# Up products of a weight chunk in two runs of one width each, and another order of the last twelve blocks of down products

## The reference

```python
# first block: one layer, D_FF = 4096
h2 = rmsnorm(x, g_mlp[i])
u = jax.nn.relu(jnp.einsum("bsd,df->bsf", h2, w_up[i]))
x = x + jnp.einsum("bsf,fd->bsd", u * u, w_down[i])
...
# second block: two such layers in each of its two layers, D_FF_2 = 2816
def swiglu(h, w_in, w_out):
    a, b = jnp.split(h @ w_in, 2, axis=-1)
    return (jax.nn.silu(a) * b) @ w_out

x = x + 0.5 * swiglu(rmsnorm_2(x, g[0]), ffn_w_in[layer, 0], ffn_w_out[layer, 0])
...
return rmsnorm_2(x, final_norm_g)
```

## Time and profile before

| | us |
|---|---|
| median of 3 runs | 1401.23 (1399.37 to 1402.98) |
| the profiled execution's own time | 1400.86 |
| its span, first to last instruction | 1398.7 |
| TensorE busy in it | 1358.7 (97%), 7680 products |
| VectorE busy | 971.6 (69%) |
| ScalarE busy | 677.3 (48%) |

### The profile page before, as it was taken

How to read it: one execution, slowest core, us unless ns; L and a number is a source line. 1 busy time by engine, 2 the same in 40 slices (tenths; PEclk the granted TensorE clock), 3 DMA queues, 4 the chain that set the end, 5 groups by cost and what they waited for, 6 DMA issues and landing times.

```text
span 1398.7 us, 19406 instructions
## 1 busy us (share of the span) xinstructions
PE 1358.7 (97%) x7680; PEld 1158.8 (83%) x7680; DVE 971.6 (69%) x1324; ACT 677.3 (48%) x1056; POOL 73.6 (5%) x113
## 2 busy tenths in 40 slices
PE   8999999999999999998999999999999988999997
PEld 6888988888888888887888888888888866888886
DVE  5886686666687667558577667776666677576664
ACT  6576444443554444455554444444444456444442
POOL 0300010000000000003000000000000143000000
PEclk9999999999999999999999999999999989999999
DMA  9443555555446555454346555465554543465551
GB/s 320 142 133 109 181 187 205 189 190 191 164 164 215 189 200 170 162 169 140 121 151 216 199 186 179 156 208 183 192 189 142 162 131 99 152 212 192 181 183 44
DMA packets 67738, 241.31 MB, mean 173 GB/s; under 512 B 8015, under 2 KB 8408, under 8 KB 67648
## 3 DMA queue, kind: packets, MB, share of 16 engines
q1 hardware_dynamic: 65344, 234.19, 50.5%
q0 software_dynamic: 2016, 5.77, 1.6%
q10 hardware_dynamic: 288, 0.11, 0.0%
HBM read 238.88 MB, written 1.09 MB: 172 GB/s over the span
## 4 chain that ended last, share of the span: by engine, by line
PE 85%; DVE 7%; ACT 3%; DMA 2%; issue 2%; POOL 1%; DVEq 0%; ACTq 0%; POOLq 0%
PE pp L457 83%; DVE wlo L1652 2%; PE pp L466 2%; DMA raw<-w_chunks 1%; ACT whi L1214 1%; DVE hx L1660 1%; DVE fa L1652 1%; ACT pbuf L1365 0%; DMA fa<-f_rows 0%; DMA gns<-gains 0%; DVE fa L1752 0%; DVE fa L1649 0%; DVE pbuf L1656 0%; DVE fa L1660 0%; ACT hx L1215 0%
## 5 line engine op out<-in xcount | busy, mean ns | idle before, releaser
L457 PE MATMUL pp<-hx,whi 128*128 128x512 f32 (+1 forms) x2400 | 733.6, 366 | 6.0 <-DVE hx L1660 3.1
L1652 DVE TENSOR_TENSOR wlo<-raw,whi 128x1024 fp32r<-128x1024 f32 (+1 forms) x445 | 522.6, 1214 | 148.7 <-ACT whi L1214 148.6
L457 PE MATMUL pp<-hx,wlo 128*128 128x256 f32 x2032 | 571.9, 281 | 0.0
L457 PEld LDWEIGHTS pp<-hx,whi 128*128 128x128 f32 x2400 | 428.8, 190 | 90.9 <-issue 7.6
L1214 ACT ACTIVATE whi<-raw 128x1024 fp32r<-128x1024 f32 (+1 forms) x445 | 442.2, 1041 | 100.5 <-PE pp L457 91.7
L457 PEld LDWEIGHTS pp<-hx,wlo 128*128 128x128 f32 x2032 | 385.6, 190 | 1.9
L457 PE MATMUL pp<-whi,ra 128*128 128x512 f32 x1144 | 367.3, 392 | 1.4 <-DVE ra L1652 1.4
L457 PEld LDWEIGHTS pp<-whi,ra 128*128 128x128 f32 x1144 | 214.6, 188 | 48.6 <-issue 2.7
L457 PE MATMUL pp<-wlo,ra 128*128 128x512 f32 x572 | 222.7, 389 | 0.0
L1752 DVE TENSOR_REDUCE fa<-pp 128x512 f32<-128x1024 f32 x104 | 126.9, 1220 | 81.3 <-PE pp L457 81.2
L1214 ACT ACTIVATE ra<-fa 128x512 fp32r<-128x512 f32 x63 | 39.8, 632 | 230.0 <-DVE fa L1660 230.0
(11 more groups left out here) (174 smaller groups left out, 780.3 us busy)
## 6 DMA issues: line engine op xcount, KB each, us to landing
raw<-w_chunks SPq DMA_DIRECT2D x437, 512.0 KB, 5.0
fa<-t_rows POOLq DMA_DIRECT2D x16, 128.0 KB, 3.5
raw<-w_chunks SPq DMA_DIRECT2D x5, 256.0 KB, 5.5
fx<-x_t SPq DMA_DIRECT2D x2, 512.0 KB, 4.7
X<-x_in SPq DMA_DIRECT2D x2, 512.0 KB, 8.1
fa<-g_fin POOLq DMA_DIRECT2D x2, 512.0 KB, 4.3
fa<-f_rows POOLq DMA_DIRECT2D x8, 128.0 KB, 3.2
cst<-consts POOLq DMA_DIRECT2D x1, 576.0 KB, 8.1
```

The lines of the kernel that those rows point to most:

```text
L457: return pe.matmul(o, lhs, rhs, start=first, stop=last, skip_group_check=True)
L1652: return dve.tensor_tensor(o, a, b, op)
```

## The change

`up_part` issues the same 32 products, but no longer by turns. First come all those that move 512 columns (`whi`, both blocks f), then all those that move 256 (`wlo`, both blocks). `opening` calls it for half chunks or quarters, so there the runs are of 8 or 4. The semaphore at the chunk's end is on the last product in both versions.

`last_end` gets the blocks in another order. The groups 8 and 9 of the first token half come first, for both column halves, and only then group 10 of both. The second token half follows, column half by column half, as before.

```diff
                 for f in range(2):
-                    o = ps[b + f]
                     for k in ks:
                         c = k * 256 + f * 128
-                        mm(o[:, :], whi[:, s, c:c + 128], flat(hx[:, k, :, :]), k == 0, False)
-                        y = mm(o[:, 0:256], wlo[:, s, c:c + 128], hh[:, k, :], False, k == 7)
+                        mm(ps[b + f][:, :], whi[:, s, c:c + 128], flat(hx[:, k, :, :]), k == 0, False)
+                for f in range(2):
+                    for k in ks:
+                        c = k * 256 + f * 128
+                        y = mm(ps[b + f][:, 0:256], wlo[:, s, c:c + 128], hh[:, k, :], False, k == 7)
                 return y
...
             def last_end(tag, base):
-                for t in range(2):
-                    for c in range(2):
-                        for g in range(8, 11):
-                            i = IDX[f"{tag}{g}"]
-                            s = i % NHL
-                            weights_ready(i)
-                            pe.wait_ge(s_ul, base + g + 1)
-                            u2 = [a[:, g % 3, :].rearrange("p (k c) -> p k c", k=2) for a in (uh, ul)]
-                            for k in range(2):
-                                a = k * 1024 + c * 512
-                                y = mm3(accs[t][c], u2[0][:, k, tk(t)], u2[1][:, k, tk(t)], whi[:, s, a:a + 512],
-                                        wlo[:, s, a:a + 512], False, (g, k) == (10, 1))
-                            if (t, c) == (1, 1):
-                                y.then_inc(s_done)
-                        if (t, c) != (1, 1):
-                            y.then_inc(s_c0)
+                def quarter(g, t, c):
+                    i = IDX[f"{tag}{g}"]
+                    s = i % NHL
+                    weights_ready(i)
+                    pe.wait_ge(s_ul, base + g + 1)
+                    u2 = [a[:, g % 3, :].rearrange("p (k c) -> p k c", k=2) for a in (uh, ul)]
+                    for k in range(2):
+                        a = k * 1024 + c * 512
+                        y = mm3(accs[t][c], u2[0][:, k, tk(t)], u2[1][:, k, tk(t)], whi[:, s, a:a + 512],
+                                wlo[:, s, a:a + 512], False, (g, k) == (10, 1))
+                    return y
+
+                for c in range(2):
+                    quarter(8, 0, c)
+                    quarter(9, 0, c)
+                quarter(10, 0, 0).then_inc(s_c0)
+                quarter(10, 0, 1).then_inc(s_c0)
+                quarter(8, 1, 0)
+                quarter(9, 1, 0)
+                quarter(10, 1, 0).then_inc(s_c0)
+                quarter(8, 1, 1).then_inc(s_done)
+                quarter(9, 1, 1).then_inc(s_done)
+                quarter(10, 1, 1).then_inc(s_done)
```

## The result

| | before | after |
|---|---|---|
| median, us | 1401.74 (4 runs, 1399.37 to 1402.98) | 1392.62 (4 runs, 1389.79 to 1392.83) |
| ratio | | 0.9927, 95% interval 0.9913 to 0.9941 |
| profiled execution, its own time | 1400.86 | 1392.83 |
| span | 1398.7 | 1390.7 |

The kernel became faster by about 0.7%, 9 us by the medians. The forecast was 1387.8 with a range of 1384 to 1396: the right way, inside the range, and about 5 us too fast (where these 5 us lie is worked out further down).

A forecast was written before the change was run, and what follows sets the result against it. TensorE's product spacing was taken to bound the feed-forward layers. Gains of 12.2 (chunks) and 1.6 (end) made 13.8, less 0.4 gave 13.4 off 1400.86: 1387.5, stated as a 1387.8 us median; range 1384 to 1396.

The forecast's parts named there:

- What bounds the kernel: Feed-forward layers: time is the number of TensorE products times their start-to-start distance; TensorE busy 97% of the span.
- Rival D: Up chunks: TensorE comes to wait for VectorE's 5.88 us cycle; 1389.9 us if only at layers' ends; within forecast's 0.78.
- That changing the width costs: Up chunks: a 512/256 pair takes 0.3528 us by turns, against 0.3467 as the sum of separate streams.
- Rival A: Up chunks: order is worth nothing, a chunk keeps 5.645 us; only the end gains, 1399.6 us; chance 0.08.
- C: Up chunks: 512-column `hx` by `whi` products stay slow in runs, chunk 5.76 us; slower, 1410.4 us; chance 0.05.
- 16 x 0.118 for the 256s: Up chunks: the run of 16 products of 256 columns takes 0.118 us each, 1.888 us together.
- the 12.2 of the sum: Up chunks: 94 chunks each save 0.130 us by grouping products of one width, 12.2 us in all.
- the 0.4 that had been taken off: Openings and mixers: 0.4 us of the gain may be absorbed where TensorE follows other engines.
- The borders: Feed-forward groups: 44 `fb` chunks pay 0.027 us each, 36 down chunks lose 0.033 each; 1.2 us each way, cancelling.
- Rival B: Up chunks: part of the gain, 256s at 0.120 us and a 0.06 border per chunk; 1396.0 us; chance 0.09.
- The end: `last_end`: four blocks ahead of group 10 remove TensorE's wait for `ul`, 1.6 us; the end moves with TensorE.
- The mixers: Mixers: drops of the clock may add 1 to 2 us either way.

The follow-up runs named there:

- the run lengths: Changed kernel with same-width runs of 2, 4 or 8 products in `up_part` instead of 16: ratios to the kernel before 0.9911, 0.9961 and 0.9935.
- the one-width kernel: `wlo` products also move 512 columns, by turns with `whi` as in the kernel before; `last_end` as in the changed kernel: 1563.42 us, one run.
- part one alone: Kernel before with only the order inside `up_part` changed, old `last_end` kept: median 1393.5 us, ratio to the kernel before 0.9939.

## Why the prediction was right, and where it was off

- *What bounds the kernel*: right. The feed-forward layers are as long as their products' distances; no other engine or transfer came to hold TensorE there. Rival D cost nothing in the changed kernel, and 0.3 us where the end still waited.
- *That changing the width costs*: right for the ordinary chunks, and shown there by the run lengths and by the one-width kernel. Rival A is out (a chunk has 5.54 us, not 5.64), and so is C: 512s of `hx` by `whi` in a run are 0.2269 us apart, below its 0.2328. As a rule it goes too far. The pairs at 0.346 by turns, which rival A had for it, are real and stay unexplained: 30 of them in one opening pay nothing, with VectorE busier than beside the pairs that pay. And the sum of two borders didn't hold for runs of 2 and 4. The formula that the prediction took from the Trainium skill as a rule against the change stands there for an isolated matmul (TensorE: Matmul & The Clock Gate, Back-to-back issue gap). The estimate of 325 ns a pair by it lies under every pair measured here, 347 and 353 ns.
- *16 x 0.118 for the 256s*: this term was sized wrong. In a run of one kind they take 0.1194 on average: 0.113 for the first, and 0.120 from then on. The 0.118 came from a stream of a mixer with three products to a slice, right behind a 512 stream, and isn't the price of a run. A chunk so saves 0.10 us and not 0.130. 94 x 0.10 = 9.4, against the 12.2 of the sum; the runs show 11.01 - 1.66 = 9.35. The value 0.120 stood in the prediction as the other bound, with 0.098 us for a chunk, and it would have given the right sum. Of the 4.8 us between the forecast and the median after, this term is 2.8, less the 0.4 that had been taken off for the openings and mixers; 0.5 is that the median before is now 1401.74 and not 1401.23; and 1.9 is left for what lies outside the feed-forward layers (0.8 by the ratio).
- *The borders*: right in size and in their balance. `fb` pays 0.03 us, and a down chunk has 5.47 us and not 5.50. Rival B, which paid 0.06 for each, is out.
- *The end*: right, 1.64 us foreseen and 1.66 to 1.67 measured; the chain behind it moved with it. `ul` of group 10 came 4.4 us from the beginning of the end, earlier than the 4.7 that was allowed for. What the sum didn't have is that part one alone makes this wait 0.3 us longer; with both parts it costs nothing.
- *The mixers*: allowed for at 1 to 2 us either way in the range, and 3.0 us against the change in this pair of profiles. By the ratio (1401.74 x 0.0073 = 10.2 us) most of it isn't there on the mean of the runs.

## What to carry to other kernels

Where TensorE is dense, try the order of products inside a chunk: here it took 0.10 us off 5.64 without a new instruction. Put products of one width in a run, and let neighbouring chunks meet with the same width (0.03 us for a border here). First look at what the pairs by turns take in your own timeline, since some pay nothing for it. Take the price of a product from a long stream of that very kind, and keep the value from a mixed stream as a bound. A wait for the last group before the end is covered by whatever independent blocks can be put ahead of it, as long as the chain behind the last product isn't made longer.

## What the runs showed of the hardware that was not expected

- In a steady stream, products of 512 columns are 0.2267 us apart and of 256 columns 0.120, whichever tile is stationary or moves. By turns, a pair takes 0.3528 in the ordinary groups and not 0.3467, but 0.3467 for 30 pairs of an opening in the same kernel, under a heavier load of VectorE. Behind a run of 256, the first five 512s take 0.028 us more together.
- The extra time isn't steady in the length of the runs: a chunk takes 5.645, 5.565, 5.60, 5.57 and 5.555 us with runs of 1, 2, 4, 8 and 16.
- The same mixer takes 116.7 to 118.6 us in ten profiles with the same instructions, shortest at a granted clock of 1.00 (116.7 to 116.9) and longest at 0.97 (118.2 to 118.6).
